# Loads of the second dense stage issued ahead of the second context's, and row blocks of the last recurrent head placed behind the products of each halving

## The reference

```python
o_ctx, o_lat = _even_mixer(...)                       # gated linear attention + softmax attention
x_lat = x_lat + m_lat[2] * _rms(o_lat @ w_out, norm_post_mix[l])
x_lat = x_lat + m_lat[5] * _rms(_swiglu(h_lat, w_gate, w_up, w_down), norm_post_ffn[l])
# layer 1, latent tokens only behind the mixer:
q, k, i = silu(fq), 1 - exp(log_f), fi                # 8 heads, two directions
S_t = diag(exp(g_t)) S_{t-1} + k_t v_t^T ; o_t = S_t^T q_t
o_lat = rms(o_fwd + o_bwd, out_norm) * silu(og)
x_lat = x_lat + m_lat[2] * _rms(o_lat @ odd_w_out, ...)
x_lat = x_lat + m_lat[5] * _rms(_swiglu(...), ...)
# second block: its own context ctx_2, mixer of latent attention and retention, a squared-relu layer, an S5 layer
```

## Time and profile before

| | us |
|---|---|
| median of 3 runs (lowest, highest) | 2656.68 (2653.49, 2658.74) |
| profiled execution | 2659.77 |
| its span | 2658.0 |
| TensorE busy | 2367.1 |
| VectorE busy | 1477.3 |
| ScalarE busy | 1036.2 |
| GpSimd busy | 211.0 |

### The profile page before, as it was taken

One profiled execution on the slowest core, in us unless ns is written; L12 is line 12 of the kernel. 1 busy time (PEld: TensorE's weight loads), 2 busy tenths in 40 slices (PEclk: granted clock), 3 DMA queues, 4 the chain that ended last, 5 costly groups with the idle time before them and its releaser, 6 DMA issues.

```text
span 2658.0 us, 35101 instructions
## 1 busy us (share of the span) xinstructions
PE 2367.1 (89%) x14706; PEld 1865.0 (70%) x14706; DVE 1477.3 (56%) x2327; ACT 1036.2 (39%) x1742; POOL 211.0 (8%) x294
## 2 busy tenths in 40 slices
PE   5987788999997988876998998989999998979999
PEld 3844455888884766665997763357788787757999
DVE  5337746555555477774454315555566554871444
ACT  3234444222224355543444435544322323321543
POOL 0001200000000033320000002100201100000110
PEclk8988999999998999997998999999999998989999
DMA  7144642434421554323653213432444333252453
GB/s 262 64 176 185 251 159 71 153 136 155 143 104 60 153 163 147 127 95 128 193 178 119 95 68 127 161 141 89 143 150 149 135 131 132 109 203 95 159 177 125
DMA packets 174846, 372.78 MB, mean 140 GB/s; under 512 B 8384, under 2 KB 101824, under 8 KB 160480
## 3 DMA queue, kind: packets, MB, share of 16 engines
q1 hardware_dynamic: 174688, 370.53, 39.8%
HBM read 340.07 MB, written 30.44 MB: 139 GB/s over the span
## 4 chain that ended last, share of the span: by engine, by line
PE 72%; DVE 14%; ACT 7%; DMA 4%; issue 2%; POOL 0%; SPq 0%; DVEq 0%; ACTq 0%
PE ps L169 71%; DVE sb_R L200 5%; ACT sb_R L248 2%; DVE sb_WP L200 1%; DMA sb_slot<-mod_w 1%; DMA sb_R<-mod_w 1%; DVE sb_H L200 1%; DVE sb_R L232 1%; PE ps L179 1%; DVE sb_X L217 1%; DVE sb_cst L214 1%; DVE sb_R L229 1%; DVE sb_cst L200 1%; ACT L244 1%; ACT sb_R L254 1%
## 5 line engine op out<-in xcount | busy, mean ns | idle before, releaser
L169 PE MATMUL ps<-sb_HP,sb_WP 128*128 128x512 f32 (+1 forms) x5736 | 1094.7, 352 | 61.2 <-DVE sb_HP L200 29.6
L169 PEld LDWEIGHTS ps<-sb_HP,sb_WP 128*128 128x128 f32 x5736 | 929.1, 193 | 211.3 <-DVE sb_HP L200 33.7
L200 DVE TENSOR_TENSOR sb_WP<-sb_slot,sb_WP 128x1024 fp32r<-128x1024 f32 x364 | 449.3, 1239 | 675.3 <-ACT sb_WP L254 675.2
L254 ACT ACTIVATE sb_WP<-sb_slot 128x1024 fp32r<-128x1024 f32 x364 | 383.0, 1057 | 820.3 <-PE ps L169 787.6
L169 PE MATMUL ps<-sb_XP,sb_WP 128*128 128x512 f32 (+1 forms) x2592 | 450.8, 336 | 10.2 <-DVE sb_XP L200 10.2
L169 PEld LDWEIGHTS ps<-sb_XP,sb_WP 128*128 128x128 f32 x2592 | 398.5, 190 | 62.5 <-DVE sb_XP L200 12.2
L200 POOL TENSOR_TENSOR sb_R<-sb_R 128x128 f32<-128x128 f32 (+2 forms) x194 | 156.4, 829 | 1823.1 <-ACT sb_R L248 1408.9
L200 DVE TENSOR_TENSOR sb_R<-sb_R 128x256 f32<-128x256 f32 (+3 forms) x398 | 200.0, 537 | 28.3 <-ACT sb_R L248 25.3
L169 PE MATMUL ps<-sb_R 128*32 128x64 f32 (+8 forms) x2088 | 167.8, 285 | 52.2 <-DVE sb_R L200 21.0
L169 PEld LDWEIGHTS ps<-sb_R 128*32 128x32 f32 (+5 forms) x2088 | 119.0, 149 | 109.6 <-issue 60.0
L248 ACT ACTIVATE sb_R<-ps 128x512 f32<-128x512 f32 (+1 forms) x208 | 99.5, 514 | 128.4 <-PE ps L169 124.9
(11 more groups left out here) (136 smaller groups left out, 1941.8 us busy)
## 6 DMA issues: line engine op xcount, KB each, us to landing
sb_slot<-mlp_w SPq DMA_DIRECT2D x32, 2048.0 KB, 8.9
sb_slot<-mod_w SPq DMA_DIRECT2D x22, 2048.0 KB, 8.6
sb_R<-ada_w SPq DMA_DIRECT2D x12, 2048.0 KB, 7.7
sb_slot<-ada_w SPq DMA_DIRECT2D x24, 1024.0 KB, 4.9
sb_slot<-ffn_w_gate SPq DMA_DIRECT2D x22, 1024.0 KB, 5.3
sb_slot<-ffn_w_up SPq DMA_DIRECT2D x22, 1024.0 KB, 7.8
sb_slot<-ffn_w_down SPq DMA_DIRECT2D x10, 2048.0 KB, 7.7
sb_slot<-odd_w_in SPq DMA_DIRECT2D x32, 512.0 KB, 7.2
```

Of the source, the lines that this page charges most:

```text
L169: return self.e.matmul(out, w, x, start=start, stop=stop, skip_group_check=True)
L200: return BLANK if self.e is None else self.e.tensor_tensor(out, a, b, op)
L254: return self.e.activation(out, a, ACT.Copy) if scale is None else self.e.activation(out, a, ACT.Copy, scale=scale)
```

## The change

Three things. SyncE issues the first two loads of `ffn1` ahead of the second context and its constants. In the last recurrent head the row blocks stand behind the diagonal and behind each halving's product; their pieces are made one step later (two pieces, not three, in the steps of head 6), and operand block 0 with the clearing comes in the last step of head 6. In the first row block of the projections of `even` and `mla`, tile 7 comes last.

```diff
-        ts = tuple(range(KT)) if k or self.down.banks else (3, 4, 5, 7, 0, 1, 2, 6)
+        ts = tuple(range(KT)) if k or self.down.banks else (3, 4, 5, 0, 1, 2, 6, 7)
...
         for n in range(2):
             self.pieces.load(sp.on(self.name), n)
+        if self.meanwhile:
+            self.meanwhile(sp)
...
-    def out_first(self, some, e):
-        for _ in range(8):
+    def out_act(self, act, h):
+        if h == 6:
+            for _ in range(8):
+                yield
+            for x in range(2):
+                self.out.some_act(act, (x,), ())
+                yield
+            self.out.some_act(act, (), (0,))
             yield
-        for x in range(3):
-            some(e, (x,), ())
+        if h == 7:
+            for k in range(7):
+                self.out.some_act(act, (k + 2,), (k + 1,) if k < 6 else ())
+                yield
+
+    def out_dve(self, dve, h):
+        if h == 6:
+            for _ in range(8):
+                yield
+            for x in range(2):
+                self.out.some_dve(dve, (x,), ())
+                yield
+            e = dve.on("odd.out")
+            e.wait_ge("made", 7, 3, of="odd.in")
+            e.fill(self.p.HP[:, :, 0, TC:T].bitcast(F32)).then_inc(*e.sig("zeros"))
+            self.out.some_dve(dve, (), (0,))
             yield
-
-    def out_act(self, act):
-        self.out.some_act(act, (), (0,))
-        for k in range(7):
-            self.out.some_act(act, (k + 3,), (k + 1,) if k < 6 else ())
-            yield
-
-    def out_dve(self, dve):
-        e = dve.on("odd.out")
-        e.wait_ge("made", 7, 3, of="odd.in")
-        e.fill(self.p.HP[:, :, 0, TC:T].bitcast(F32)).then_inc(*e.sig("zeros"))
-        self.out.some_dve(dve, (), (0,))
-        for k in range(7):
-            self.out.some_dve(dve, (k + 3,), (k + 1,) if k < 6 else ())
-            yield
+        if h == 7:
+            for k in range(7):
+                self.out.some_dve(dve, (k + 2,), (k + 1,) if k < 6 else ())
+                yield
...
-            together(self.project_pe(pe, h + 1) if h < 7 else self.out_pe(pe), self.mix_pe(pe, h), self.read_pe(pe, h - 1), steps(more, 11))
+            together(*([self.project_pe(pe, h + 1)] if h < 7 else []), self.mix_pe(pe, h), self.read_pe(pe, h - 1),
+                     *([self.out_pe(pe)] if h == 7 else []), steps(more, 11))
...
+    ffn1.meanwhile = mla.early_sp
...
-            if stage is ffn1:
-                mla.early_sp(sp)
```

## The result

The changed kernel took 2625.05 us (median of four executions, 2619.69 to 2628.52) where the kernel before took 2655.41 beside it: a ratio of 0.9883, 95% interval 0.9862 to 0.9903. The same kernel once more, with five executions, gave 2629.33 and 0.9903 [0.9884, 0.9921]. The nine together have a median of 2628.54 against 2655.84 for the 13 of before beside them: 27.3 us less. The forecast was 23.9 less (2633, range 2624 to 2643).

The account below looks back on a forecast made before the run. TensorE, busy 89% of 2658.0 us, was taken as the bound, so only its idle or half-clock time counts. Terms −15.0 − 5.0 − 4.3 + 0.4 = −23.9 from 2656.7 gave 2633 us, range 2624 to 2643.

Parts of the forecast that it names:

- The loads: Before the second dense stage: first weights issued earlier, ScalarE's whole transfer wait goes; −15.0 us, bounds −15.5 and −13.0.
- R3: Less idle time lets row block 0 and the dense stage's first blocks run at 2.4 GHz; −28, 2628; chance 0.15.
- The head: Last recurrent head: earlier diagonal and row blocks behind products gain 5.0 us; bounds −7 and +1.
- Step (a): Last head: diagonal moves ahead of row block 0; VectorE reaches it at about 1165.5 instead of 1172.11, 6.6 us earlier.
- Step (b): Last head: one weight piece (1.2 us) now falls behind the diagonal, leaving −5.4 of −6.6.
- step (c): End of last head: products 5 and 6 no longer follow both last row blocks; −5.6, or −4.1 with one at half clock.
- The banks: First mixer's output projection: bank 7 last removes most of TensorE's 2.56 us stop; −4.3 us, bounds −4.7 and −2.4.
- The step on the clock: First mixer's output projection: half clock goes with the stop, giving −4.3; were it independent, −2.4.
- The second mixer: Second mixer's output projection: bank 0, now fourth, isn't free in time; TensorE waits, +0.4 us, between 0 and +0.8.
- R1: Last head gives nothing: row blocks behind products expose each product's wait; gain 18.9, 2638; chance 0.15.
- R2: Second dense stage: only the load order helps, not the earlier start; 7.4 us instead of 15.0, 2640; chance 0.06.
- R4: Last head becomes a serial chain of row blocks, products and VectorE, so slower: +13.6, 2670; chance 0.03.

## Why the forecast was right, and where it was short

**The loads: −15.0 forecast, −16.07 measured.** The mechanism held at each step: the pairs are issued in the head, both land before it ends, no wait is left, and what is late next is the chain of pieces, low parts and additions. It was given 9.21 us from the first piece to the norm, and takes 1203.86 − 1195.61 = 8.25. The 0.96 is the ones-products: they took 2.08 at half clock after 16 us of standing, and now

```profile
1202.69 1.13 PE L169 MATMUL ps<-sb_H,sb_cst 128*128 128x256 f32 x4 [0.98 <-DVE sb_H L200]
```

The old length of a part behind a wait was carried over, though the wait was what had slowed it. The clock was thought of as rival R3 only, and there at the row blocks; row block 7 stayed at 5.49.

**The head: −5.0 forecast, −7.33 measured.** Step (a) held: VectorE reaches the diagonal at

```profile
1158.03 0.41 DVE L217 SCALAR_TENSOR_TENSOR sb_R<-ps,sb_cst 128x256 f32<-128x256 f32 x1
```

without a wait, 8.77 us after head 6's values; before it was 1172.11 − 1157.12 = 14.99, so 6.2 sooner (forecast 6.6). Step (b) failed: "one weight piece (1.2) now falls behind that point". It does fall behind the diagonal, but not ahead of operand 5, on which row block 5 waits. The VectorE rows up to there:

```profile
1177.01 1.22 DVE L200 TENSOR_TENSOR sb_WP<-sb_slot,sb_WP 128x1024 fp32r<-128x1024 f32 x1
1178.14 0.42 DVE L200 TENSOR_TENSOR sb_HP<-sb_H,sb_HP 128x256 fp32r<-128x256 f32 x1
...
1179.81 1.22 DVE L200 TENSOR_TENSOR sb_WP<-sb_slot,sb_WP 128x1024 fp32r<-128x1024 f32 x1
```

Between diagonal and operand 5 (1178.14) stand pieces 3 to 6, four of them; before these were 4 to 7, four too. VectorE's waits between the two points are 2.4 us, where they were 3.0, which is the rest of the difference. The added one, piece 7, comes at 1179.81, where TensorE has 3.11 us of row block 5 to do. So operand 5 comes 6.85 sooner (measured from head 6's values), not 5.4, and with it the last product, 6.97 sooner against 5.6 in step (c). The other 0.4 to 7.33 lies between that product and row block 7. The sum took 0.6 off again, from −5.6 to −5.0, for a row block at half clock; none of the six was.

**The banks: −4.3 forecast, −4.34 measured, and 2.1 more elsewhere.** The step on the clock was right. By the idle time alone the term was 2.4; that the half clock behind the stop would go with it gave 4.3. The prediction had weighed here what the Trainium skill says ("TensorE: Matmul & The Clock Gate", section "What's actually happening"): the throttled clock is the default, and activity releases it. The trace agrees: the stop went, and so did the 0.50. What was not forecast is that the same kind of gain appears twice more, 1.2 and 0.9, behind other stops later in the program.

**The second mixer: +0.4 forecast, +0.14 measured**, inside its bounds.

With the right sizes the sum is −16.07 − 7.33 − 4.34 − 2.1 + 0.14 = −29.7. The parts alone give 15.1, 8.0 and 6.6: 29.7 too, so within the 5 us or so that the three intervals leave together they add without helping or hindering each other. The table says it more finely: each edit's own stretch gains the same alone and in the whole. The two medians of the changed kernel are 30.4 and 26.5 below before, the pooled one 27.3; the intervals of the ratios hold 29.7 in both. Why the pooled median is 2 us short of it isn't settled; the start alone varies by 9 us between profiles.

**The rivals.** R1 is refuted by the head alone (−8.0). R2 is refuted as the outcome, its price near: 7.4 forecast (7.8 with the bytes counted right), 6.85 measured when only the order was changed. The Trainium skill ("DMA: Bandwidth & Descriptors", section "Queues, rings and completion order") says that each DMA engine takes its descriptors in ring order. The trace agrees: with those bytes no longer ahead, the weights landed that much sooner. R3 (28 less) came nearest to the time but not by its mechanism: it had the row blocks of the second dense stage at full clock, and the gain came in the ones-products and the first dense stage. Row block 0 of the head did get shorter, 5.30 for 6.67, inside the head's term. R4 is real, and one step away: with the pieces three ahead all of the head's gain is gone. Against it the prediction said that "VectorE's weight pieces run three ahead, so most of the chain is free of the row block". That was the wrong way round: it is being three ahead, in a ring of four, that ties the piece to the row block, and the change's step back to two that frees it.

## What to carry to other kernels

When a product and bulk work are interleaved on TensorE, look at what the bulk work's release lets go on the other engines, and in which place of their order that stands: running further ahead in a ring is only safe while the entry that must be free was finished before the product at hand. When a stop is removed, price the work behind it at full clock as well, and look for a second cover before a remaining cost is attacked: here the half clock of row block 7 and the pieces hid each other, and neither edit alone brought more than 0.13 us. An added instruction costs only if it stands ahead of the one that is waited for; count them between those two points in both orders, not behind one of them.

## What was not expected of the hardware

A stop that is removed in one place moved the clock in others: with the new banks the half clock behind a 4.5 us stop, 65 us later in the same code, ended so much sooner that 29 matmuls ran in 8.25 us instead of 24, with a gain of 1.2 to 1.4 us in all eight profiles with the edit and of 0.3 at most in the four without. The time at half clock had only moved, into a stretch in which TensorE waits anyway. And identical code ran its four ones-matmuls in 1.13 us in two profiles and in 2.08 in a third, so that a stretch of 8.57 us was 9.51.
